# A hybrid decoder layer in FP32 on one NeuronCore: gate projections by seven products over twelve of their sixteen row tiles

## What is computed

```python
h = rms_norm(x, g_attn[l])
proj = h @ w_in[l]
qa, ka, va, fa, qb, kb, vb, ga, gb = jnp.split(proj, offs, axis=-1)
...
merged = jax.nn.sigmoid(ga) * (o_a @ w_br_fox[l]) + jax.nn.sigmoid(gb) * (o_b @ w_br_dil[l])
x = x + merged @ w_out[l]
h = rms_norm(x, g_ffn[l])
u = h @ w_up[l]
...
x = x + (jax.nn.silu(gate) * val) @ w_down[l]
```

## Time and profile before

| | us |
|---|---|
| median of 3 runs | 1337.79 (1337.57 to 1338.55) |
| the profiled execution | 1338.0 |
| its span | 1336.1 |
| PE busy | 1330.0 |
| DVE busy | 1121.9 |
| ACT busy | 940.9 |

### The profile page before, as it was taken

One profiled execution on the slowest core, in us unless ns is written; L12 is line 12 of the kernel. 1 busy time (PEld: TensorE's weight loads), 2 busy tenths in 40 slices (PEclk: granted clock), 3 DMA queues, 4 the chain that ended last, 5 costly groups with the idle time before them and its releaser, 6 DMA issues.

```text
span 1336.1 us, 16447 instructions
## 1 busy us (share of the span) xinstructions
PE 1330.0 (100%) x6055; PEld 1101.8 (82%) x6055; DVE 1121.9 (84%) x1333; ACT 940.9 (70%) x1180; POOL 156.2 (12%) x175
## 2 busy tenths in 40 slices
PE   9999999999999999999999999999999999999999
PEld 7888888888888888888878888888888888888887
DVE  6768787888888876657789898999999999999996
ACT  6666666666666654446777778888888888888872
POOL 0121212021011000001010102011111102020200
PEclk9999999999999999999999999999999999999999
DMA  9868685758888655667879798999989999999952
GB/s 353 286 167 265 141 259 119 241 155 230 237 216 228 206 175 172 211 227 226 272 172 327 155 306 172 312 220 286 243 259 264 230 283 218 302 208 311 201 195 103
DMA packets 118175, 305.73 MB, mean 229 GB/s; under 512 B 11848, under 2 KB 13136, under 8 KB 117584
## 3 DMA queue, kind: packets, MB, share of 16 engines
q1 hardware_dynamic: 92288, 234.57, 50.6%
q0 software_dynamic: 21728, 66.07, 28.0%
q10 hardware_dynamic: 4080, 4.05, 0.9%
HBM read 302.55 MB, written 2.11 MB: 228 GB/s over the span
## 4 chain that ended last, share of the span: by engine, by line
PE 98%; ACT 1%; DMA 0%; issue 0%; DVE 0%; SPq 0%; ACTq 0%
PE acc L741 14%; PE acc L745 14%; PE acc L743 13%; PE acc L779 9%; PE acc L783 9%; PE acc L781 9%; PE acc L964 4%; PE acc L960 4%; PE acc L962 4%; PE acc L937 3%; PE acc L939 3%; PE acc L935 3%; PE acc L1072 1%; PE acc L765 1%; PE acc L761 1%; PE acc L763 1%
## 5 line engine op out<-in xcount | busy, mean ns | idle before, releaser
L1754 DVE TENSOR_TENSOR w_lo<-raw,w_hi 128x1024 fp32r<-128x1024 f32 x234 | 283.9, 1221 | 89.4 <-ACT w_hi L1240 88.2
L1240 ACT ACTIVATE w_hi<-raw 128x1024 fp32r<-128x1024 f32 x234 | 244.7, 1054 | 108.4 <-PE acc L745 77.8
L741 PE MATMUL acc<-w_hi,actA 128*128 128x512 f32 x664 | 261.5, 394 | 0.1
L745 PE MATMUL acc<-w_hi,actA 128*128 128x512 f32 x664 | 258.9, 390 | 0.0
L743 PE MATMUL acc<-w_lo,actA 128*128 128x512 f32 x664 | 258.5, 389 | 0.0
L1240 ACT ACTIVATE w_hi<-raw_y 128x1024 fp32r<-128x1024 f32 x144 | 149.7, 1058 | 71.1 <-PE acc L745 22.0
L1754 DVE TENSOR_TENSOR w_lo<-raw_y,w_hi 128x1024 fp32r<-128x1024 f32 x144 | 173.3, 1220 | 23.4 <-ACT w_hi L1240 22.0
L1754 DVE TENSOR_TENSOR w_lo<-raw_x,w_hi 128x1024 fp32r<-128x1024 f32 x108 | 130.1, 1221 | 42.6 <-ACT w_hi L1240 42.5
L745 PEld LDWEIGHTS acc<-w_hi,actA 128*128 128x128 f32 x664 | 124.6, 188 | 26.4
L741 PEld LDWEIGHTS acc<-w_hi,actA 128*128 128x128 f32 x664 | 124.7, 188 | 25.9 <-issue 1.1
L743 PEld LDWEIGHTS acc<-w_lo,actA 128*128 128x128 f32 x664 | 124.8, 188 | 25.2
(11 more groups left out here) (296 smaller groups left out, 2598.6 us busy)
## 6 DMA issues: line engine op xcount, KB each, us to landing
raw<-w_in SPq DMA_DIRECT2D x102, 512.0 KB, 4.8
raw<-w_down SPq DMA_DIRECT2D x59, 512.0 KB, 5.6
raw_x<-w_up SPq DMA_DIRECT2D x44, 512.0 KB, 5.0
raw_y<-w_up POOLq DMA_DIRECT2D x34, 512.0 KB, 7.7
raw_x<-w_in SPq DMA_DIRECT2D x28, 512.0 KB, 4.1
raw<-w_out SPq DMA_DIRECT2D x28, 512.0 KB, 4.5
odd<-w_up SPq DMA_DIRECT2D x27, 512.0 KB, 5.3
work<-w_up SPq DMA_DIRECT2D x24, 512.0 KB, 5.4
```

What stands on the lines that cost most here:

```text
L741: nc.tensor.matmul(o, lhsT=a_h, rhs=w_hi[:, s, k, :], start=first and k == 0, stop=False, skip_group_check=onto_seed)
L745: mm = nc.tensor.matmul(o, lhsT=a_l, rhs=w_hi[:, s, k, :], start=False, stop=last and k == KU - 1, skip_group_check=onto_seed)
L1240: nc.scalar.activation(w_hi[:, n % RING, :, :], src.rearrange("p (k n) -> p k n", k=KU), ACT.Copy).then_inc(hi_done, 1)
L1754: nc.vector.tensor_tensor(w_lo[:, n % RING, :, :], src.rearrange("p (k n) -> p k n", k=KU), w_hi[:, n % RING, :, :].bitcast(f32), ALU.subt ...
```

## The change

Rounds 3 to 6 use three quads in place of two: 12 of the 16 row tiles go by seven products, and 4 by plain units. `gate_units` in the new order:

```diff
+        if c >= QK:
+            units += some("P3", 0) + some("P1", 0) + some("P3", 1) + some("P1", 1, 2) + some("P3", 2)
+            units += some("P7", 0, 1) + some("P6", 0) + some("P7", 2) + some("P6", 1, 2)
+            units += plain(0, 0) + some("P5", 0, 1) + plain(0, 1) + some("P5", 2) + plain(1, 0)
+            units += some("P2", 0, 1) + some("P4", 0, 1) + some("P2", 2) + plain(1, 1) + some("P4", 2)
+            continue
         units += product("P3") + plain(0, 0) + product("P1") + plain(0, 1) + product("P7")
         units += product("P6") + plain(0, 2) + product("P5") + plain(0, 3) + plain(1, 0)
         units += product("P2") + plain(1, 1) + product("P4") + plain(1, 2) + plain(1, 3)
```

The third quad's buffers: `gate_y(2)` is `tmp`, `gate_x(c, 2)` a free part of `gb` in round 3 and `softmax` afterwards. Since `softmax` also holds POOL's `prep`, the preparation of head 12 moves behind the last round:

```diff
+                third_sum(c, QU)
+                for q in range(QU + 1):
+                    first_sum(c, q)
+            pool.wait_ge(y_added[QU], 2 * gate_uses(QU))
+            for c in range(4):
                 prepare_dil(12 + c).then_inc(prep_ready, 1)
```

C11 is no longer gathered by DVE. ACT copies the negated P1 into `bank[2]`, the plain units of side 0 and P2 run on in that bank, and ACT's sigmoid reads it there:

```diff
+                if unit == ("H", c, "P1", QU):
+                    act.wait_ge(used, n + 1)
...
+                    nc.scalar.activation(bank[2], bank[0], ACT.Copy, scale=-1.0).then_inc(g_p1, 1)
...
+                if r == 0:
+                    act.wait_ge(used, GATE_AT["H", QK + c, "P2", QU] + 1)
+                    act.wait_ge(used, GATE_AT[last_plain(QK + c, 0)] + 1)
+                    cols = slice(c * NB, (c + 1) * NB)
+                    nc.scalar.activation(ga[:, 0, cols], bank[2], ACT.Sigmoid, scale=xrs[:, 0:1]).then_inc(g_c11, 1)
```

The places of the copies and sums are in tables now, as distances in units:

```diff
+SUM_C22_AT, SUM_C21_AT = (1, ("H", "P3", 0)), (1, ("H", "P3", 0))
+SUM_C12_AT, SUM_V7_AT = (0, ("G", 1, 1)), (0, ("G", 0, 0))
+SIGMOID_AT = (("H", "P3", 0), ("G", 0, 0))
+COPY_AHEAD = {("H", "P1", QU): 0, ("H", "P6", QU): 2, ("H", "P5", QU): 1, ("G", 1, 1): -1}
```

`COPY_AHEAD` 0 puts ACT's copy at its unit, before `high(n + 6)`; 1 or 2 that many units earlier in ACT's program; -1 one unit later. Branch start on PE and DVE:

```diff
                 if c == 0:
-                    pe.wait_ge(g_c11, PAIRS)
+                    pe.wait_ge(g_c12, PAIRS - 1)
                     pe.wait_ge(g_c21, PAIRS)
...
                     if c == 0 and u == 0:
                         dve.wait_ge(g_u1, PAIRS)
                         gate_rest(gb[:, 1, 3 * NB:4 * NB])
+                        dve.wait_ge(used, BR_UNIT)
+                        dve.wait_ge(g_v7, PAIRS)
+                        gate_result(bank[3], ga[:, 1, 3 * NB:4 * NB], g_c21)
```

More of the change, by code:

```diff
@@ L47, in first_block, with gate_quads, gate_uses, gate_use @@
     return 0 if q < QU else FULL if q < QX - 1 else WHOLE
+def gate_quads(c):
+    return QU if c < QK else QU + 1
+def gate_uses(q):
+    return PAIRS if q < QU else PAIRS - QK if q == QU else 0
+def gate_use(c, q):
+    return c if q < QU else c - QK
 def uses_before(i, q):
[L51 removed]
+    return gate_uses(q) + i - first_block(q)
 def added_before(i, q):
[L56 to L57 removed]
+    return 2 * gate_uses(q) + sum(1 if fourth_by_transfer(b, q) else 2 for b in range(first_block(q), i))
 def by_transfer_before(i, q):
@@ L110 @@
 GATE_PARTS = ("P3", "P5", "P6")
+WIDE_PARTS = ("P3", "P5", "P6")
 def raw_use(n):
@@ L1493, in _ @@
                 gate_sum(n, unit)
-                if unit[2] == "P6" and unit[3] == QU - 1:
-                    high(n - 1 + RING)
-                if unit[2] != "P6" or unit[3] == QU - 1:
-                    high(n + RING)
+                for ahead in (2, 1, 0, -1):
+                    m = n + ahead
+                    if m < BR_UNIT and GATES[m - GATE_UNIT][1] >= QK:
+                        if COPY_AHEAD.get(place(GATES[m - GATE_UNIT])) == ahead:
+                            wide_copies(m, GATES[m - GATE_UNIT])
+                if unit[1] >= QK:
+                    high(n + RING)
+                else:
+                    if unit[2] == "P6" and unit[3] == QU - 1:
+                        high(n - 1 + RING)
+                    if unit[2] != "P6" or unit[3] == QU - 1:
+                        high(n + RING)
+                wide_high(unit)
                 c, at = unit[1], place(unit)
@@ L2029, in gate_rest, with wide_sums @@
                 nc.vector.tensor_tensor(to, to, bank[7], ALU.subtract).then_inc(g_c22, 1)
+            def wide_sums(n, unit):
+                for c in (unit[1], unit[1] - 1):
+                    if not QK <= c < PAIRS:
+                        continue
+                    second_bank = gate_banks(c)[1]
+                    at = (unit[1] - c, place(unit))
+                    if at == SUM_V7_AT:
+                        dve.wait_ge(g_v, c + 1)
+                        gate_result(bank[7], pair_sum(c, 0, 1), g_v7)
+                    if at == SUM_C12_AT:
+                        dve.wait_ge(used, GATE_AT[last_plain(c, 1)] + 1)
+                        dve.wait_ge(g_u0, c + 1)
+                        gate_result(bank[second_bank], pair_sum(c, 1, 0), g_c12)
+                    if at == SUM_C22_AT:
+                        dve.wait_ge(g_u1, c + 1)
+                        gate_rest(pair_sum(c, 1, 1))
+                    if at == SUM_C21_AT:
+                        dve.wait_ge(used, GATE_AT["H", c, "P4", QU] + 1)
+                        dve.wait_ge(g_v7, c + 1)
+                        gate_result(bank[3], pair_sum(c, 0, 1), g_c21)
@@ L2034, in gate_bank_sums @@
                 first_bank, second_bank = gate_banks(c)
-                if unit == ("H", c, "P3", 0) and c > QK:
-                    dve.wait_ge(g_u1, c)
-                    gate_rest(pair_sum(c - 1, 1, 1))
+                if c >= QK:
+                    wide_sums(n, unit)
                 elif unit == ("G", c, 0, 2):
```

249 lines of the change are left out of this document (176 added, 73 removed).

## The result

| | before | after |
|---|---|---|
| median, us | 1337.72 | 1351.88 |
| all runs, us | 1337.57 to 1338.55 | 1350.80 to 1355.98 |
| ratio, 95% interval | | 1.0110 (1.0098 to 1.0123) |
| span of the profiled execution, us | 1336.1 | 1349.8 |

What follows compares the result with a forecast made beforehand. The prediction took PE to bound the kernel, busy 1330.0 of 1336.1 us. Its terms, -5.4 + 3.9 + 2.7 + 1.1 = +2.3 us on 1337.8, gave 1340.1 us, with an eight-in-ten range of 1335.8 to 1346.

Steps and rivals of the forecast that it cites:

- the bound on the wait for C21: End of the gates: PE's wait for the C21 sum was put between 0.9 and 4.5 us.
- the values stage at nothing: Values stage before round 3: 12 small DVE instructions, 5 us in all, were given no cost of their own there.
- -5.44 for 24 matmuls: Gate rounds: six matmuls fewer in each of four rounds, at 0.2267 us each, all on the path.
- +3.9 for the wait at the end: Branch start: PE waits 3.9 us for C21, which stands on DVE behind C12, two splits and C22.
- above: 4.5, if the last split waits for its load: End of the gates: upper bound of 4.5 us on the wait, should the last branch tile's load be late.
- POOL's preparation of head 12: Around the branch start: comes later, 1 us long, put at nothing since its user on DVE comes late.
- Rival B: Behind the end's wait: the 3.9 us wait halves PE's clock, 2.9 us lost, 1343.0 us in all; chance 0.14.
- +2.7 in rounds 4 to 6: Gate rounds 4 to 6: PE waits 0.7 us at two narrow places and 0.2 at a third; bounds 0 and 8.4.
- +1.1 in round 3: Gate round 3: P3 of quad 2 is split late, so its adding transfer starts late; 1.1 us, bounds 0 and 3.
- rival A: Gate rounds: y tile's chain outlasts the round, about 2.5 us in rounds 4 to 6, 2 in round 3; 1345.8; chance 0.28.
- t0: Start of a gate round; DVE was to begin P7 at t0 + 4.7, P6 ready at t0 + 14.2, wanted at t0 + 13.6.
- the 5 us come out of slack: Values stage: the small DVE instructions' 5 us were to fit in DVE's idle time, 2.77 us of it seen after them.

Runs made afterwards that it cites:

- e1: Changed kernel with the last round's C21 sum moved on DVE from the branch start to right behind C12; 1345.06 us.
- e11: e1 with the last round's C12 and C21 sums one place earlier, ahead of DVE's split of branch tile 3; 1344.57 us.
- e2: Changed kernel with 28 unread matmuls on PE between the last gate product and the wait for C21; 1348.85 us.
- e9: e11 with round 2's eight small sums and differences made by POOL in place of DVE; 1343.63 us.
- e6: Changed kernel with DVE's additions behind P7 in rounds 4 to 6 cut to one column a row, work left out; 1345.01 us.
- e5: Changed kernel without POOL's adding transfers behind P3 of quads 0 and 1 in rounds 4 to 6, work left out; 1348.45 us.
- e7: Changed kernel with first plain unit ahead of all P7s, last round's P4 of quad 2 before its last plain unit, eight small DVE instructions spread over round 2; 1357.67 us.
- e12: e9 with, in rounds 3 to 6, the first plain unit between the first two P7 products and the second ahead of P5; 1350.79 us.
- e13: e12 with ACT's copy of P5 one place earlier, ahead of the split for P4 of quad 0; 1350.20 us.
- e14: e13 with the last round's P4 of quad 2 ahead of the last plain unit and C21 summed before branch tile 2's split; 1351.77 us.

## Why the prediction was wrong

The sign was leaned to rightly (0.48 slower, against 0.08 faster), but 1340.1 and the upper end of 1346.0 were both too low. The two steps that failed are the bound on the wait for C21 and the values stage at nothing; in the rounds the mechanism was right and its size was not. Its own steps, against the trace:

- **-5.44 for 24 matmuls:** right, and all on the path.
- **+3.9 for the wait at the end:** the mechanism was right (e1, e11), the size was half of the 7.5 measured. The step that failed is "above: 4.5, if the last split waits for its load": ACT began that split 3.6 us later than in the sum, not 0.6. Two splits stand ahead of C21, and both are of tiles whose buffers come free only when DVE, now later by its own load, has read the tiles before them. The rows on the landing of SP's loads were in hand and not applied to branch tiles 4 and 5. POOL's preparation of head 12 was put at nothing since its user comes late; that it holds up DVE by 0.6 us just there was left out.
- **Rival B, +2.9 for the clock at a chance of 0.14:** it happened (2.3 us; e2), near its price, but behind a wait of twice the length it was told for. Whether 3.9 us would have brought it no run shows: waits of 2.07 to 2.97 us brought it in six cases and did not in five (last section). Section HAM oscillation of the Trainium skill's page TensorE: Matmul & The Clock Gate says that long idle gaps of PE bring the clock down; by that rule B had to come with a wait of 7.4 us, and the trace agrees.
- **+2.7 in rounds 4 to 6, +1.1 in round 3:** 6.9 and 0.1 measured. For round 3 the mechanism did not show: the 12 small instructions delayed what stands ahead of the gates and not P3 of quad 2 by enough to hold up PE. For rounds 4 to 6 rival A came near to true at a chance of 0.28: landings of 7.7, 7.8 and 7.1 us where it wanted 8, and 2.4, 2.6 and 1.9 us a round where it had 2.5; its 2 us in round 3 did not come. The rows of round 5:

```profile
374.94 1.20 POOL L2557 DMA_DIRECT2D raw_y<-w_in  x1 [23.76 <-DVE w_lo L1895]
...
382.71 1.06 ACT L1324 ACTIVATE w_hi<-raw_y 128x1024 fp32r<-128x1024 f32 x1 [3.31 <-DMA raw_y<-w_in]
```

  The landing was 7.8 us and not 7.0, and the issue came at t0 - 2.6 and not t0 - 3.4, so DVE began P7 at t0 + 6.2 in place of t0 + 4.7. With that one value the prediction's own sum, 6.2 + 9.56 - 13.6, gives 2.2 us, where 2.6 were measured. The text took the middle one of three landings seen at a DMA share of 0.88.
- **The values stage at nothing:** it cost 2.3 us. The step that failed is "the 5 us come out of slack": the idle time of 2.77 us lies at the stage's end, and what PE waits for in it is not a split but the softmax and the head norm, which stand behind the new instructions in DVE's queue. e9's trace shows it; its median alone (0.9 us below e11's) would not.
- **The range:** the end (+3.6), the clock (+2.3), the rounds (+3.2) and the values stage (+2.3) all erred the same way, 11.4 us in all. The range let one rival come true at a time, and B and most of A both did. It seems that they are not independent, since a fuller DVE can lengthen each of them: with DVE's additions cut in e6 the wait at the end fell as well, from 7.4 to 6.5 us. That is a reading, no run tests it by itself.

What stays open: whether the 5 us of waits in the rounds of the changed order can be removed at all without lightening DVE or the transfers. Leaving work out does it (e5, e6), and three new orders only moved them or doubled them (e7, e12, e13), which fits a chain that closes on itself through the two buffers of a quad. Why an adding transfer lands after 6 us in one execution and 8 in another is open as well. A run that cuts that chain with a further buffer wasn't tried, nor was one that shows why the orders of e12 to e14 have twice the waits.
